# The last feed-forward products by halves of the tokens, and the last norm with a token in a partition

## What is computed

```python
hn = rms_norm_2(h, ffn_norm_g[l])
h = h + (jax.nn.silu(hn @ w_ffn_gate[l]) * (hn @ w_ffn_up[l])) @ w_ffn_down[l]
y = rms_norm_2(h, final_norm_g)
return y[:, PAD + N_META:]
```

## Time and profile before

| what | value |
|---|---|
| runs | 1576.21, 1576.78, 1579.12 us, median 1576.78 |
| profiled execution | 1577.14 us, its span 1575.3 us |
| TensorE | busy 1527.1 us, 97% of the span, 7198 matmul records |
| VectorE, ScalarE, GpSimd | busy 821.4, 618.1 and 351.3 us |
| granted TensorE clock | 0.989 in the mean |
| TensorE's share of the chain that ended last | 86% |

### The profile page before, as it was taken

The page is one execution under the profiler, slowest core; times in us unless marked ns, Lnnn a source line. Parts: engine busy times, 40 slices in busy tenths (PEclk is TensorE's granted clock), DMA queues, the critical chain, the costliest instruction groups (busy, mean ns, idle before and its releaser), DMA issues.

```text
span 1575.3 us, 19521 instructions
## 1 busy us (share of the span) xinstructions
PE 1527.1 (97%) x7198; PEld 1213.0 (77%) x7202; DVE 821.4 (52%) x1644; ACT 618.1 (39%) x1119; POOL 351.3 (22%) x364
## 2 busy tenths in 40 slices
PE   7999999999999999999999999999999999999995
PEld 5786666788888888888888788866688888888884
DVE  5556676344455343433446697587365443443444
ACT  5433577332244132322446343566443322321223
POOL 3300455100020000000036524445531210210112
PEclk9999899999999999999999999999999999999998
DMA  5763100433232333333322653312432333333321
GB/s 194 137 156 112 43 15 1 135 105 94 80 108 86 102 93 94 94 95 104 95 88 68 165 150 115 114 48 81 135 105 79 99 104 94 94 95 105 94 81 53
DMA packets 46685, 154.11 MB, mean 98 GB/s; under 512 B 5714, under 2 KB 5906, under 8 KB 46592
## 3 DMA queue, kind: packets, MB, share of 16 engines
q1 hardware_dynamic: 41856, 137.63, 27.9%
q0 software_dynamic: 4736, 15.25, 4.6%
HBM read 142.78 MB, written 9.55 MB: 97 GB/s over the span
## 4 chain that ended last, share of the span: by engine, by line
PE 86%; DVE 8%; ACT 3%; issue 2%; DMA 1%; DVEq 0%; another core or an unknown queue 0%; POOL 0%; SPq 0%; ACTq 0%
PE PSA L581 84%; PE PSA L786 2%; DVE AR L1797 1%; DVE AR L1795 1%; ACT AR L1309 1%; DVE WL L1707 0%; DMA XT<-xT_in 0%; DVE AHL L1913 0%; ACT AHL L1358 0%; PE PSA L930 0%; DVE AR L2293 0%; DVE AR L2386 0%; DVE AR L1913 0%; ACT WH L1237 0%; DVE AR L1736 0%
## 5 line engine op out<-in xcount | busy, mean ns | idle before, releaser
L581 PE MATMUL PSA<-Ah,WH 128*128 128x512 f32 x1072 | 424.7, 396 | 13.1 <-DVE Al L1716 9.0
L581 PE MATMUL PSA<-Ah,WL 128*128 128x512 f32 x1072 | 419.4, 391 | 0.0
L581 PE MATMUL PSA<-Al,WH 128*128 128x512 f32 x1072 | 419.3, 391 | 0.0
L1237 ACT CAST WH<-WR 128x1024 fp32r<-128x1024 f32 (+3 forms) x234 | 240.9, 1031 | 227.6 <-PE PSA L581 216.8
L1707 DVE TENSOR_TENSOR WL<-WR,WH 128x1024 fp32r<-128x1024 f32 (+3 forms) x207 | 254.9, 1232 | 86.5 <-ACT WH L1237 86.2
L581 PEld LDWEIGHTS PSA<-Ah,WH 128*128 128x128 f32 x1072 | 202.4, 189 | 62.4 <-issue 18.5
L581 PEld LDWEIGHTS PSA<-Ah,WL 128*128 128x128 f32 x1072 | 202.3, 189 | 42.8
L581 PEld LDWEIGHTS PSA<-Al,WH 128*128 128x128 f32 x1072 | 202.5, 189 | 41.9 <-issue 0.7
L581 PE MATMUL PSA<-Bh,WH 128*128 128x512 f32 (+1 forms) x592 | 230.4, 389 | 4.1 <-DVE Bl L1984 2.3
L581 PE MATMUL PSA<-Bh,WL 128*128 128x512 f32 (+1 forms) x592 | 229.1, 387 | 0.0
L581 PE MATMUL PSA<-Bl,WH 128*128 128x512 f32 (+1 forms) x584 | 226.5, 388 | 0.0
(11 more groups left out here) (364 smaller groups left out, 1916.0 us busy)
## 6 DMA issues: line engine op xcount, KB each, us to landing
WR<-w_in SPq DMA_DIRECT2D x228, 512.0 KB, 3.6
gt_tmp<-AR SPq DMA_DIRECT2D x16, 256.0 KB, 2.2
WR<-w_in SPq DMA_DIRECT2D x8, 384.0 KB, 3.1
XT<-scr_tmp POOLq DMA_DIRECT2D x8, 264.0 KB, 12.3
XT<-scr_tmp POOLq DMA_DIRECT2D x8, 256.0 KB, 15.2
XT<-xT_in POOLq DMA_DIRECT2D x1, 2048.0 KB, 9.6
x_tmp<-XT POOLq DMA_DIRECT2D x1, 2048.0 KB, 7.5
AHL<-gt_tmp SPq DMA_DIRECT2D x8, 256.0 KB, 4.0
```

Source lines behind the costliest of these rows:

```text
L581: return pe.matmul(o, l, r, start=start, stop=stop)
L1237: ac.copy(WH[p][:, 0:n], WR[j % RAW][:, 0:n]).then_inc(w_hi, 1)
```

## The change

- TensorE's last eight down products are made twice, for tokens 0 to 255 and then for 256 to 511, with matmuls of 256 columns. The first two products of the first half are interleaved.
- For this all eight fd tiles of the third chunk must stay. The last five (fd 19 to 23) have their halves written to `Ah` and `Al`, the gate and up products' input, which is free once the last up product is complete; their casts wait for that alone.
- The last norm is made in the same halves, `fin0` and `fin1`: four matmuls with a column of ones give the sums with a token in a partition (128 partitions, 2 columns), variance, Sqrt, reciprocal and Newton step go over 2 columns, and two matmuls spread the root over the partitions of a bank, from which VectorE scales all eight pieces of a half. GpSimd scales none. The first half's output is made and sent during the second half's products: 16 transfers of 128 KB.
- A table load for Sqrt is placed behind the fifth square of the first half; Ln and Exp of the last norm go.
- In VectorE's program the call `split_to(tid["fu", m] + 2)` behind the gate product is gone. In the loops over the down tiles of all chunks `split_to` stands ahead of the wait for the product, where it stood behind the add.

```diff
+        KEPT = {tid["fd", 19 + i]: i for i in range(5)}
+        def halves(j):
+            if j in KEPT:
+                return [X[:, :, :].rearrange("p k t -> p (k t)")[:, KN * KEPT[j]:KN * KEPT[j] + KN] for X in (Ah, Al)]
+            return WH[(hi_no[j] - 1) % SPL], WL[(hi_no[j] - 1) % SPL]
...
# SyncE
+            for n, (nm, k) in enumerate([(nm, k) for nm in COLS for k in range(8)]):
+                sp.wait_ge(n_g, n + 1)
+                sp.dma_start(out[k, :, COLS[nm]], OUT[:, k, COLS[nm]]).then_inc(d_out[k % 2], 16)
...
# TensorE
+                if nm in COLS:
+                    for a in range(2):
+                        for x in (NP[nm][0], NP[nm][1][0]):
+                            last = mm(sums_at(nm)[:, a:a + 1], x[:, 128 * a:128 * a + 128], ONE[:, 0:1], x is NP[nm][0], x is not NP[nm][0])
+                    last.then_inc(n_ps.sem, 1)
+                    return
...
+            def spread(nm):
+                pe.wait_ge(n_nr.sem, n_nr.end(nm))
+                for a in range(2):
+                    last = mm(roots_at(nm)[:, 128 * a:128 * a + 128], NP[nm][5][:, a:a + 1].to_broadcast([128, 128]), ident, True, True)
+                last.then_inc(n_rc, 1)
...
+            pe.wait_ge(u_ad, 16)
+            ws = [halves_ready(tid["fd", 16 + i]) for i in range(2)]
+            for k in range(n):
+                ready(k)
+                for i in range(2):
+                    last = chunk(ws[i], hC[0], k, bank(6 + i)[:, 0:256], n)
+                    if k == n - 1:
+                        last.then_inc(u_h0, 1)
+            for m in range(2, 16):
+                pe.wait_ge(u_ad, 15 + m)
+                if m == 9:
+                    sums("fin0")
+                if m == 10:
+                    spread("fin0")
+                ws = halves_ready(tid["fd", 16 + m % 8])
+                for k in range(n):
+                    last = chunk(ws, hC[m // 8], k, bank(6 + m % 2)[:, 0:256], n)
+                last.then_inc(w_mm if m > 7 else u_h0, 1)
+            sums("fin1")
+            spread("fin1")
...
# ScalarE, down loop of the third chunk
                     split_to(tid["fd", 8 * ci + i] + 2)
                     if ci == 2:
                         ac.wait_ge(u_ad, 17 + i)
-                        square("fin", i)
-                        if 4 < i < 7:
-                            with_gain(i)
+                        square("fin0", i)
+                        if i == 4:
+                            ac.activation(NS[:, 24:25], ONE[:, 0:1], ACT.Sqrt)
...
+            for i in range(8):
+                ac.wait_ge(u_ad, 25 + i)
+                square("fin1", i)
+                if i == 0:
+                    column_root("fin0")
+            column_root("fin1")
...
# VectorE, gate and up loop
                     dv.scalar_tensor_tensor(out=RT[2 * s + 1], in0=TH[s], scalar=0.5, in1=bank(b + 1), op0=ALU.mult,
                                             op1=ALU.mult).then_inc(u_t3, 1)
-                    if m:
-                        split_to(tid["fu", m] + 2)
                     dv.wait_ge(u_hi, m + 1)
...
# VectorE, down loops
                 for i in range(8):
-                    result(tid["fd", 8 * ci + i])
-                    dv.tensor_tensor(x3[:, i, 0:T], bank(6 + i % 2), x3[:, i, 0:T], ALU.add).then_inc(u_ad, 1)
+                    x = x3[:, i, 0:T] if ci < 2 else x3[:, i, COLS["fin0"]]
                     split_to(tid["fd", 8 * ci + i] + 2)
+                    if ci < 2:
+                        result(tid["fd", 8 * ci + i])
+                    else:
+                        dv.wait_ge(u_h0, i + 1)
+                    dv.tensor_tensor(x, bank(6 + i % 2)[:, 0:T if ci < 2 else 256], x, ALU.add).then_inc(u_ad, 1)
...
+            for i in range(8):
+                result(tid["fd", 16 + i])
+                x = x3[:, i, COLS["fin1"]]
+                dv.tensor_tensor(x, bank(6 + i % 2)[:, 0:256], x, ALU.add).then_inc(u_ad, 1)
+                if i == 0:
+                    variance("fin0")
+                    column_newton("fin0")
+                if 0 < i < 5:
+                    for k in range(2 * i - 2, 2 * i):
+                        normed("fin0", k)
+            variance("fin1")
+            column_newton("fin1")
+            for k in range(8):
+                normed("fin1", k)
```

More of the change, by code:

```diff
@@ L268, in build, with sums_at, roots_at @@
         ckh, ckl = Bh[:, 6:8, :].rearrange("p a t -> p (a t)"), Bl[:, 6:8, :].rearrange("p a t -> p (a t)")
+        def sums_at(nm):
+            return bank(0 if nm == "fin0" else 1)[:, 0:2] if nm in COLS else bank(6)
+        def roots_at(nm):
+            return bank(2 if nm == "fin0" else 3)[:, 0:256]
         hA = (lambda k: Ah[:, k, :], lambda k: Al[:, k, :])
@@ L570, in sync_program @@
                 weights(j)
[L571 to L576, removed]
+            for n, (nm, k) in enumerate([(nm, k) for nm in COLS for k in range(8)]):
+                sp.wait_ge(n_g, n + 1)
+                sp.dma_start(out[k, :, COLS[nm]], OUT[:, k, COLS[nm]]).then_inc(d_out[k % 2], 16)
+            sp.wait_ge(d_out[0], 128)
+            sp.wait_ge(d_out[1], 128)
         def tensor_program(pe):
@@ L1219, in tensor_program @@
                 f += n
-            sums("fin")
+            hC = [(lambda k, c=c: Bh[:, k, c], lambda k, c=c: Bl[:, k, c]) for c in COLS.values()]
+            pe.wait_ge(u_ad, 16)
[18 more added lines that the diff above has]
+            spread("fin1")
         def scalar_program(ac):
@@ L1232, in split_to @@
                         continue
-                    n, p = tiles[j][2], (hi_no[j] - 1) % SPL
+                    n = tiles[j][2]
                     ac.wait_ge(w_ld[j % RAW], 16 * (j // RAW + 1))
-                    if hi_no[j] > SPL:
+                    if j in KEPT:
+                        result(tid["fu", sum(SIZES2) - 1])
+                    elif hi_no[j] > SPL:
                         ac.wait_ge(w_mm, mm_no[by_hi[hi_no[j] - SPL]])
-                    ac.copy(WH[p][:, 0:n], WR[j % RAW][:, 0:n]).then_inc(w_hi, 1)
+                    ac.copy(halves(j)[0][:, 0:n], WR[j % RAW][:, 0:n]).then_inc(w_hi, 1)
             def result(j, r=0):
@@ L1704, in split_to @@
                         continue
-                    n, p = tiles[j][2], (hi_no[j] - 1) % SPL
+                    n, (wh, wl) = tiles[j][2], halves(j)
                     dv.wait_ge(w_hi, hi_no[j])
-                    dv.tensor_tensor(WL[p][:, 0:n], WR[j % RAW][:, 0:n], WH[p][:, 0:n].bitcast(F),
-                                     ALU.subtract).then_inc(w_lo, 1)
+                    dv.tensor_tensor(wl[:, 0:n], WR[j % RAW][:, 0:n], wh[:, 0:n].bitcast(F), ALU.subtract).then_inc(w_lo, 1)
             def result(j, r=0):
@@ L2378, in vector_program, with column_newton, normed @@
                 for i in range(8):
-                    result(tid["fd", 8 * ci + i])
-                    dv.tensor_tensor(x3[:, i, 0:T], bank(6 + i % 2), x3[:, i, 0:T], ALU.add).then_inc(u_ad, 1)
+                    x = x3[:, i, 0:T] if ci < 2 else x3[:, i, COLS["fin0"]]
                     split_to(tid["fd", 8 * ci + i] + 2)
-                f += n
[L2383 to L2386, removed]
-                                        op0=ALU.mult, op1=ALU.mult).then_inc(n_g, 1)
+                    if ci < 2:
[3 more added lines that the diff above has]
+                    dv.tensor_tensor(x, bank(6 + i % 2)[:, 0:T if ci < 2 else 256], x, ALU.add).then_inc(u_ad, 1)
+                f += n
+            def column_newton(nm):
+                r = NP[nm][3]
+                dv.wait_ge(n_r.sem, n_r.at(nm, 0))
+                dv.reciprocal(r, r).then_inc(n_r.sem, 1)
+                newton(nm)
+            def normed(nm, k):
+                if k == 0:
+                    dv.wait_ge(n_rc, 3 if nm == "fin0" else 4)
+                dv.scalar_tensor_tensor(out=OUT[:, k, COLS[nm]], in0=x3[:, k, COLS[nm]], scalar=gv[4][:, k:k + 1], in1=roots_at(nm),
+                                        op0=ALU.mult, op1=ALU.mult).then_inc(n_g, 1)
+            for i in range(8):
[12 more added lines that the diff above has]
+                normed("fin1", k)
         def pool_program(pl):
@@ L2563, in pool_program @@
                 pl.tensor_tensor(ZR[s], RT[2 * s], RB["m2"], ALU.mult).then_inc(u_zr, 1)
[L2564 to L2568, removed]
+            for nm in COLS:
+                add_squares(nm)
         with nc.Block() as block:
```

39 lines of the change are left out of this document (22 added, 17 removed).

## The result

The changed kernel took 1632.67 us (median of 4 runs, 1631.26 to 1635.78), the kernel before 1576.49 us beside it (4 runs, 1574.98 to 1579.12): a ratio of 1.0354, with a 95% interval of 1.0338 to 1.037. The forecast was 1617.1 us with a range of 1611 to 1624. The sign was right and the size was not: the change costs about 56 us where I had 40. In the later comparisons two executions ran at a lower granted clock throughout, one of the kernel before (1869.2 us) and the profiled one of the version with the later table load (2548.07 us): the ratios leave them out, and that trace is not read.

A forecast was written before the change was run, and what follows sets the result against it. TensorE was taken to bound the kernel, so only its waits and the tail count. 40.3 + 3.3 + 1.6 + 3.7 + 1.2 - 9.8 = +40.3 us on 1576.8 gave 1617.1 us, range 1611 to 1624.

The forecast's parts named there:

- What bounds the kernel: Whole kernel: TensorE, 86% of the span; time counts only in its waits or behind its last product (19.8 us).
- The stalls of the loop: Gate and up loop: fu m subtracted too late in 18 steps, 2.24 us each, +40.3 us.
- the clock falls in the stalls: Rival, gate and up loop: slow matmuls behind each stall, 32 us more, 1649 us; chance 0.04.
- one gap of 2.9 us: Near the kernel's start, about 125 us: granted clock 1.00 behind a TensorE gap, used as evidence against clock falls.
- The beat of 0.43 us: Sign, behind the 18 waits of the loop: matmuls at this beat would show the forecast wrong.
- The start of the last down chunk: Ahead of fd 16: interleaved products need fd 17 at once, but it is subtracted later; +3.3 us.
- Half the tokens per product: Last down products: 288 matmuls of 256 columns at 0.119 us replace 144 of 512; +1.6 us.
- The first half's chain: Last down chunk, first half: ring, interleaved pair's wait and Sqrt table load delay TensorE; +3.7 us.
- the ring: First half of last down products: add, square, cast, subtraction, next add take 2.49 us against TensorE's 2.14.
- Sums and spread: First half's norm on TensorE: four float32 matmuls for sums and two spreads; +1.2 us.
- The tail: From the last product's last matmul to the span's end: 10.0 us against 19.8, -9.8 us.
- The sum of the last stage: Behind the gate and up loop: +9.8 us of costs meet -9.8 us of tail, coming out even.

The follow-up runs named there:

- the version with the later table load: Changed kernel with both split_to calls ahead of VectorE's waits and Sqrt's table load behind the seventh square, not the fifth: 1571.98 us, ratio 0.9972.
- the loop with the gaps filled: Changed kernel with nine unread 512-column matmuls between fg m and fu m in the 18 stalling steps: 1620.44 us, ratio 1.0276; loop alone 360.85 us.
- that with 16-column matmuls: Changed kernel with 18 unread matmuls of 16 columns filling the gap between fg m and fu m: 1631.95 us, ratio 1.035.

## Why the prediction was wrong, step by step

- **What bounds the kernel**: right. The difference is in TensorE's waits, in its beat, or behind its last product.
- **The stalls of the loop**: right in number (18), place, cause and length (2.39 us). The 2.16 us each above a beat are 39.0 us, and the restart was 0.12 us in place of 0.08. Forecast 40.3; without the falls it is 18 x 2.28 = 41.0, and the loop with the gaps filled, where the clock does not fall, is 40.9 longer than before. The second subtraction of each call ends 2.2 us behind the first and not 1.14, beside GpSimd's product; nothing waits for it.
- **The clock: the step that failed.** The sum has it at nothing, and the rival "the clock falls in the stalls" stood at 0.04, on one gap of 2.9 us with a clock of 1.00 behind it. The fall does happen, behind six of the eighteen stalls, eight matmuls at 0.43 in place of 0.23 us each time, 1.6 us and some 1.7 with the restart. The loop took 50.7 us more: 39.0 for the gaps, and 11.7 for six falls and twelve restarts. I had made it all or nothing, 0 or 32 us, and given all my weight to nothing; one gap cannot tell "never" from "one in three". The beat of 0.43 us, which the prediction named as a sign that it is wrong, is what came. The removal by filling (9.8 us less in the loop with 512 columns, none with 16) shows that this is the clock and no other cost of the stall.
- **The one gap itself was an exception.** The row of the granted clock lies inside the gap, where TensorE does nothing. And the same gap, in a part of the program that the change leaves alone, loses the clock in the changed kernel's own trace (matmuls, then the stretch with its granted clock):

  ```profile
  125.17 0.39 PE L604 MATMUL PSA<-Ah,WL 128*128 128x512 f32 x1
  128.05 0.47 PE L604 MATMUL PSA<-Ah,WH 128*128 128x512 f32 x1 [2.49 <-DVE WL L1776]
  128.00:132.00 4.00, 3.95 (x11) 0.57 0.37 131
  ```

  Of the eleven profiled executions read here the clock falls behind this gap of 2.9 us in nine; only that of the kernel before and that with 16-column matmuls keep it. So the row on which the sum rested was one draw, and an unlucky one.
- **The warning was in the trace of before.** In the kernel before, matmuls of 512 columns are on the lower level about 1 us behind 24 matmuls of 16 columns, 0.11 us apart with no idleness (columns as above):

```profile
852.00:853.00 1.00, 1.00 (x5) 0.72 0.47 188
853.00:854.00 1.00, 1.00 (x4) 0.50 0.00 0
```

  The narrow ones start at 848.67 and the last at 851.15. The same 24 are followed by a fall in four of the eleven executions. A look at all stretches with a clock under 1.00, and not only at the one gap, would have found it. The same stretch of program, then, loses the clock in one execution and keeps it in another. The Trainium skill, "TensorE: Matmul & The Clock Gate", Part 1, says that the number of slow matmuls at a kernel's start, before the clock has risen, differs from run to run of the same kernel. The traces agree: records of over 0.6 us are the first seven of the kernel before and the first fourteen of the changed one, whose programs are alike there. No run here shows what decides which gap loses the clock.
- **The start of the last down chunk**: 3.49 us against 3.3, right. But a fall of the clock follows it as well, fifteen matmuls of 256 columns at 0.21 in place of 0.12 us, 1.4 us. It was in the range, not in the sum.
- **Half the tokens per product**: right, a beat of 0.12 us against 0.119.
- **The first half's chain**: the ring is 2.50 us against 2.49, and the product behind the table load waits 1.6 us against 1.5. The load with its activation is over at 1596.07, 1.50 us behind its start, without a drain of its own, as the prediction had it from the row.
- **Sums and spread**: about 0.9 us against 1.2.
- **The tail**: 10.6 us against 10.0. The three runs of small work are each a little longer than I had them (sums 1.02 against 0.6).
- **The sum of the last stage**: forecast 0.0, measured +2.8 us (1574.24 to 1629.5 against 1522.83 to 1575.3). 1.4 of it is the clock, 0.6 the tail and 0.2 the gap; the remaining 0.6 is spread over terms too small to separate.
- **What stays open**: which of the 2.4 us gaps lose the clock is not settled: 5 or 6 of 18 in the kernels with that gap, 0 at 1.8, 18 at 4.6. And the first gate product of the loop starts 0.7 us later than before (1203.64 against 1202.91); this is no more than executions differ ahead of the loop, where that start lies between 1200.5 and 1207.5 us in kernels with the same work ahead of it.

The 54.2 us between the two spans are then: gaps 39.0, falls and restarts 11.7, ahead of the loop 0.7, last stage 2.8. The medians are 56.2 us apart. The other three executions of the changed kernel have a granted clock of 0.978 to 0.981 in the mean, where the profiled one has 0.983, which would fit a few more falls; they have no trace.

## What to carry to other kernels

When a call that does work up to a given tile is removed or moved, write down for each tile which remaining call does it and when the consumer wants it; a tile that is subtracted "one call later" here was late by a whole handoff in 18 steps. Price a stall of TensorE of more than 2 us at its length plus a share of a clock fall (here 1.6 us, in a third of the cases at 2.4 us and in most at 2.9), and look for every stretch of the trace with a lowered clock before putting that share at zero. One gap in one execution does not show that the clock holds: the same gap may lose it in the next. Work that another engine waits for belongs ahead of its own engine's waits: that alone turned this change from 3.5% slower to about even, and with two orders mended behind it to 0.4% faster.

## What the runs showed of the hardware

- The clock fell behind 0 of 18 gaps of 1.8 us, 5 or 6 of 18 of 2.4 us, 9 of 11 executions of one gap of 2.9 us, all six gaps of 3.7 us (ahead of fd 16, one in each of six kernels), and 18 of 18 of 4.6 us. With about 2 us of matmuls of 16 columns in the 2.4 us gaps it still fell behind 6 of 18; with matmuls of 512 columns, behind none.
- One fall cost 1.6 us: eight matmuls of 512 columns at 0.43 us. Behind the gap ahead of fd 16, fifteen of 256 columns at 0.21 us cost 1.4.
- A subtraction on VectorE with both inputs of 1024 columns in SBUF takes 1.22 us, but 2.3 us when it starts while GpSimd runs a product of its own, and then it ends 1.1 us behind the end of that product: two in a row last 3.44 us in the changed kernel. One that had started 0.16 us ahead of GpSimd's product was not slowed. No run varied GpSimd's product alone.
